# Moving operand tiles and weight-slab slots to other byte offsets within 512

## The reference

```python
h = h + 0.5 * swiglu(rmsnorm(h), w_gate, w_up, w_down)          # FFN_DIM = 2816
h = h + mixer(rmsnorm(h))   # three branches, gated and summed, then @ w_out:
#   gated linear attention (4 heads), Mamba-2 SSD (8 groups of 4 heads), chunked attention (16 heads)
h = h + 0.5 * swiglu(rmsnorm(h), w_gate2, w_up2, w_down2)
return rmsnorm(h)
```

## Time and profile before

| | before |
|---|---|
| median of three runs | 1852.97 us (1850.91 to 1854.07) |
| the profiled execution, its own time | 1850.31 us |
| its span, first to last instruction | 1848.5 us |
| what lies around the span | 1.8 us |
| mean granted TensorE clock | 0.996 |
| PE busy | 1817.7 us (98%), 9852 matmuls |
| PEld busy | 1499.5 us (81%), 9852 loads |
| DVE, ACT, POOL busy | 961.3, 622.2, 115.5 us |
| DMA | 89 GB/s on average |

### The profile page before, as it was taken

How to read it: one execution, slowest core, us unless ns; L and a number is a source line. 1 busy time by engine, 2 the same in 40 slices (tenths; PEclk the granted TensorE clock), 3 DMA queues, 4 the chain that set the end, 5 groups by cost and what they waited for, 6 DMA issues and landing times.

```text
span 1848.5 us, 26276 instructions
## 1 busy us (share of the span) xinstructions
PE 1817.7 (98%) x9852; PEld 1499.5 (81%) x9852; DVE 961.3 (52%) x1360; ACT 622.2 (34%) x986; POOL 115.5 (6%) x109
## 2 busy tenths in 40 slices
PE   7999999999999999999999999999999999999997
PEld 5888888887888888788888888887888888888885
DVE  6444443379888888532544445555334544444333
ACT  4323222234444444332233244443222323232221
POOL 4111100001101100000000000000000011111000
PEclk9999999999999999999999999999999999999998
DMA  4332223331222222222222222222232223232331
GB/s 157 100 97 96 98 95 102 102 98 62 70 68 68 79 68 68 80 92 95 88 85 75 82 89 85 84 91 69 92 98 95 91 94 99 94 99 92 109 104 58
DMA packets 47353, 164.92 MB, mean 89 GB/s; under 512 B 5520, under 2 KB 6672, under 8 KB 47296
## 3 DMA queue, kind: packets, MB, share of 16 engines
q1 hardware_dynamic: 43584, 158.10, 26.4%
q10 hardware_dynamic: 3712, 6.03, 1.1%
HBM read 162.01 MB, written 2.10 MB: 89 GB/s over the span
## 4 chain that ended last, share of the span: by engine, by line
PE 75%; issue 19%; DVE 3%; POOL 1%; ACT 1%; DMA 0%; POOLq 0%; DVEq 0%; SPq 0%; ACTq 0%
PE G L536 37%; PE G L578 12%; PE I L536 9%; PE G L552 7%; PE I L898 1%; POOL hid L458 1%; PE I L932 1%; PE I L908 1%; PE I L707 1%; PE I L715 1%; PE G L765 1%; DVE UL L1495 1%; PE I L725 1%; PE I L868 0%; PE I L872 0%
## 5 line engine op out<-in xcount | busy, mean ns | idle before, releaser
L1479 DVE TENSOR_TENSOR WL<-RAW,WH 128x1024 fp32r<-128x1024 f32 x297 | 374.1, 1262 | 309.6 <-ACT WH L1027 300.7
L1027 ACT CAST WH<-RAW 128x1024 fp32r<-128x1024 f32 x297 | 309.3, 1046 | 240.6 <-PE I L536 131.9
L536 PE MATMUL G<-UH,WH 128*128 128x512 f32 x696 | 172.9, 390 | 0.0
L536 PE MATMUL G<-UH,WL 128*128 128x512 f32 x696 | 171.9, 389 | 0.0
L536 PE MATMUL G<-UL,WH 128*128 128x512 f32 x696 | 171.8, 389 | 0.0
L536 PEld LDWEIGHTS G<-UH,WH 128*128 128x128 f32 x696 | 130.6, 188 | 28.0 <-issue 1.0
L536 PEld LDWEIGHTS G<-UL,WH 128*128 128x128 f32 x696 | 130.7, 188 | 27.1
L536 PEld LDWEIGHTS G<-UH,WL 128*128 128x128 f32 x696 | 130.7, 188 | 27.1
L536 PE MATMUL G<-NH,WH 128*128 128x512 f32 x448 | 115.5, 399 | 0.0
L536 PE MATMUL G<-NL,WH 128*128 128x512 f32 x448 | 113.6, 395 | 0.0
L536 PE MATMUL G<-NH,WL 128*128 128x512 f32 x448 | 113.6, 395 | 0.0
(11 more groups left out here) (309 smaller groups left out, 2551.4 us busy)
## 6 DMA issues: line engine op xcount, KB each, us to landing
RAW<-in_slabs SPq DMA_DIRECT2D x297, 512.0 KB, 3.3
h<-in_x SPq DMA_DIRECT2D x4, 512.0 KB, 6.4
bias<-in_rel ACTq DMA_DIRECT2D x16, 128.0 KB, 3.1
out_y<-h ACTq DMA_DIRECT2D x8, 256.0 KB, 2.2
bias<-in_rel ACTq DMA_DIRECT2D x16, 112.0 KB, 2.6
cst<-in_cst SPq DMA_DIRECT2D x1, 168.0 KB, 3.6
ut<-in_wgk SPq DMA_DIRECT2D x3, 32.0 KB, 8.3
```

The lines of the kernel that those rows point to most:

```text
L536: ins = mm(dst, W[:, n.slot, (k - k0) * P:(k - k0 + 1) * P], R[:, k, :], start=begin and which == 0 and k == k0, stop=end and which == 2 a ...
L1027: nc.scalar.copy(WH[:, n.slot, :], RAW[:, n.slot, :]).then_inc(split_hi, 1)
L1479: V.tensor_tensor(WL[:, n.slot, :], RAW[:, n.slot, :], WH[:, n.slot, :].bitcast(F32), ALU.subtract).then_inc(split_lo, 1)
```

## The change

Nothing is computed differently; instructions, their order and their semaphores stay. Only places in SBUF change:

- Every slot of `WH` and `WL` gets 16 spare elements (64 bytes) behind it. Slots are 4160 bytes apart: `WH` slots begin at 128, 192 and 256 in 512, `WL` slots at 320, 384 and 448.
- A tensor `offset` of 32 elements fills up to the next 512 bytes.
- Small tensors move (`four_eps`, `DAH`, and the attention tiles `PT2`, `mx`, `ngm`, `rs`, `rc`), so that everything fits, and so that the large operand tiles behind the tables begin at 128 in 512 in place of 160: `NH`, `NL`, `HH`, `HL`, `SL`, `AH`, `AL`, `MH`, `ML`, and also `ut`, `MSH`, `MSL`, `WGK` and the working tiles. `after_r` goes from 192 to 160 and `LR` from 352 to 320. `UH`, `UL`, `GH`, `GL`, `SH` and `RAW` stay at 128.

```diff
+STEP = 16
-        WH = sb("WH", [P, RING, SLAB], F32R)
-        WL = sb("WL", [P, RING, SLAB], F32R)
+        WH = sb("WH", [P, RING, SLAB + STEP], F32R)
+        WL = sb("WL", [P, RING, SLAB + STEP], F32R)
+        sb("offset", [P, 128 - 6 * STEP])
...
-        four_eps = sb("four_eps", [P, TT])
...
+        late = ExitStack()
+        PT2 = sb("PT2", [P, 2, 256], F32, late)
+        mx = sb("mx", [P, 2, TT], F32, late)
+        ngm = sb("ngm", [P, 2, TT], F32, late)
+        rs = sb("rs", [P, 2, TT], F32, late)
+        rc = sb("rc", [P, 2, TT], F32, late)
+        late.close()
         SC = sb("SC", [P, 32, HS])
...
+        DAH = sb("DAH", [P, TT * HS], F32R, prep)
         prep.close()
...
-        DAH = sb("DAH", [P, TT * HS], F32R, w)
+        four_eps = sb("four_eps", [P, TT], F32, w)
...
-        PT2 = sb("PT2", [P, 2, 256], F32, w)
-        mx = sb("mx", [P, 2, TT], F32, w)
-        ngm = sb("ngm", [P, 2, TT], F32, w)
-        rs = sb("rs", [P, 2, TT], F32, w)
-        rc = sb("rc", [P, 2, TT], F32, w)
...
-                nc.scalar.copy(WH[:, n.slot, :], RAW[:, n.slot, :]).then_inc(split_hi, 1)
+                nc.scalar.copy(WH[:, n.slot, 0:SLAB], RAW[:, n.slot, :]).then_inc(split_hi, 1)
...
-                V.tensor_tensor(WL[:, n.slot, :], RAW[:, n.slot, :], WH[:, n.slot, :].bitcast(F32),
+                V.tensor_tensor(WL[:, n.slot, 0:SLAB], RAW[:, n.slot, :], WH[:, n.slot, 0:SLAB].bitcast(F32),
                                 ALU.subtract).then_inc(split_lo, 1)
```

## The result

| | before | after |
|---|---|---|
| median of 16 runs each | 1851.27 us (1850.18 to 1854.07) | 1855.49 us (1854.71 to 1856.33) |
| ratio after / before | | 1.0022, 95% interval 1.0014 to 1.0030 |
| the profiled execution, its own time | 1850.31 us | 1854.89 us |
| its span | 1848.5 us | 1853.1 us |
| mean granted TensorE clock | 0.996 | 0.995 |

The change costs 4.2 us. The forecast was 1872 us, +19.0: the right side, inside the range, but more than four times the size. (Of the 16.5 us between 1872 and 1855.5, 1.7 come from the median of before, 1852.97 when the prediction was made and 1851.27 now.)

A forecast was written before the change was run, and what follows sets the result against it. PE, busy throughout, was taken to bound the kernel through its step length. +6.1 us (512 columns) and +12.9 (256 columns) made +19.0 on 1850.3, 1869.3; with 2.7 for the median, 1872 us, range 1848 to 1895.

The forecast's parts named there:

- The two-port rule: Trainium skill's rule that moving operand and weight load have independent read ports; by it the change is worth nothing.
- Step 2: 512-column matmuls: moving the operands alone brings 3392 of them from 233.5 to 226.7 ns, -23.1 us.
- the 64-byte rival: Pattern repeats every 64 bytes: 512-column steps settle at 226.7 ns, 256-column form +2.7 us; 1833 us; chance 14%.
- Step 3: 512-column matmuls: spare bytes spread the leads over 0 to 320; net with the operands' move, +6.1 us.
- lead: Stationary operand's place in 512 less the moving one's; claimed 229.0 ns at 0 and 64, 233.5 from 128 to 320.
- Step 4: 256-column matmuls of line 578: 1493 of them, off lead 0, rise to 126.6 ns; +12.9 us.
- The inference of a period of 512: Weight load and moving stream meet about once in 512 bytes, so the pattern repeats after 512, not 64, 128 or 256.
- The 256-column form doesn't care: Rival: line 578 is unmoved, its +12.9 us term nothing; +6 us in all, 1859 us; chance 16%.
- dearer: Rival: 4866 matmuls put at the dear level take 238 ns, 4.5 ns more; +22 us, 1894 us; chance 12%.
- no meeting: Rival: some middle leads of the 512-column form step at 213.3 ns; below 1805 us; chance 4%.
- Nothing: Rival: nothing to measure, as gains and losses cancel or addresses play no part; 1853 us; chance 9%.

The follow-up runs named there:

- pad_only: Changed kernel with its padded slots, but the operands behind the tables left at 160 as before; 1861.32 us, ratio 1.0052 to the kernel before.
- align_only: Changed kernel without the spare bytes: operands moved to 128, slots unpadded; 1833.77 us, ratio 0.9902 to the kernel before.
- hi0_lo64: Changed kernel without slot padding, 16 spare elements between WH and WL instead: WH slots at lead 0, WL at lead 64; 1853.13 us.
- hi0_lo192: Changed kernel without slot padding, 48 spare elements between WH and WL instead: WH slots at lead 0, WL at lead 192; 1840.46 us.

## Why the prediction was right or wrong

**What bounds the kernel: right.** All versions keep their work and their clock (0.993 to 0.996), the steps with waits in them add up to the same within 4 us, and the time follows the step. Between the two extremes, 1833.8 and 1876.6 us, nothing differs but addresses.

**The two-port rule: the trace disagrees, as said, and the runs now show it.** The Trainium skill, page TensorE: Matmul & The Clock Gate, section "Step-by-step: what each phase is for", has the weight load take nothing from the running matmul, because each has its own read port. Moving tiles alone took 1% off the kernel (0.9902), and the price goes by the place of the one operand less that of the other (`pad_only`). The same page, section "Back-to-back issue gap", gives N / 2.4 + 2.5 ns for the gap of an isolated matmul; an estimate by it is 215.8 ns for 512 columns. No settled step with 512 columns was under 226.7 here, where each matmul brings its own weight load.

**Step 2, moving the operands: right in the steps.** -23.1 us was forecast, -22.4 measured in `align_only`. The 256-column form gave +2.8, as the 64-byte rival had it (+2.7). What I left out is that waits give back some 3.6 us of the 19.6: the span fell by 16.0.

**Step 3, the spare bytes in the 512-column form: near in its sum, by errors that cancel.** +6.1 us forecast, +4.1 measured. Against what the slots measured:

- lead 0: 229.0 forecast, 229.0 measured; reading it from the earlier trace rows held.
- lead 64: 229.0 forecast, 233.4 measured: 1349 x 4.4 = 5.9 us too little. The failing reading is "its nearest row is +32, which is cheap": cheapness was taken from the shortest duration in a group of 389/482/775. Both 32 and 64 settle at 233.3.
- lead 192: 233.5 forecast, 228.6 measured, 675 x 4.9 = 3.3 us too much; lead 256: 233.5 against 231.1, 1.6 us too much. The second is lead 0, unsettled in a run of eight behind lead 64.
- lead 128 (232.8) and 320 (233.4): as forecast but for 0.9 us.
- The slots have no equal shares. The 40 slabs of the 256-column form always fall in slots 1 and 2, so slot 0, the cheap one, has 99 of the 257 others. That gives some 1.3 of the remaining 2 us.

By settled prices, with these shares, the changed kernel would have a mean of 99/257 x 227.4 + 79/257 x (231.1 + 232.9) = 230.2 ns, and the kernel before has (2680 x 226.7 + 3392 x 233.3) / 6072 = 230.4. So the set of leads that the change brings is no dearer than the old one. The measured means are 231.2 and 230.5: the changed kernel pays 1.0 ns a step for switching the lead within and between slabs, the size seen in `hi0_lo64` and `hi0_lo192`, where before paid 0.1. (0.9 ns more by 5960 steps is 5.4 us, less 0.2 x 5960 = 1.2 of the settled prices: the +4.1.) This split is worked out, from settled prices measured one by one. It was not shown by a kernel with the same leads and no switches, which can't be built.

**Step 4, the 256-column form: this is the step that failed.** +12.9 us forecast, -1.3 measured; this term is 14.2 of the 14.4 us between the +19.0 of the sum and the +4.6 of the span (step 3 is 2.0 more, and the SSD rounds, which had no term, give 1.8 the other way with the rest). Its size was 119.8 + 6.8 ns, the price that the other form pays, carried over because "the extra falls in the time of the weight load, which both forms have whole". Not one D brings the mean of this form above 119.9 ns. It even ranks them otherwise: D 0, best with 512 columns, is worst here, together with 96. Beyond the columns alone (213.3 and, at 2.4 GHz, 256 / 2.4 = 106.7 ns) D 0 costs the same 13 ns in both forms, which fits the argument; but going from D 0 to 64 adds 6.6 ns with 512 columns and takes away 2.3 with 256. So it is the extra of the other places that doesn't carry over from one form to the other. The lower bound that I had written down (118.3, costing nothing more) was still a little high. The share of lead 0 was wrong as well (none of the WH slabs, since slot 0 isn't used), but that hardly matters at prices between 117.3 and 119.9.

**The inference of a period of 512: wrong.** Lines 822 and 679 were to exclude 64, 128 and 256. The row of line 822 does exclude 64: 320 would be 0 there, and it was dear, as the runs confirm. But 128 and 256 were both excluded by "288 would be 32", and so by the misread 32. For 128 the runs bear the conclusion out all the same (232.7 ns at lead 128, 226.7 at 0); for 256 they refute it. One bad reading thus made both the wrong period and the wrong price of lead 64. The picture of a load that meets the stream once in 512 bytes falls with it.

**The rivals.** "The 256-column form doesn't care" (1859 us) was the mechanism that decided, and its change is the nearest: +6 against the 4.2 measured. That it comes so near is in part luck, since its +6 is step 3 with errors that cancel. Of the 3.5 us between 1859 and 1855.5, 1.7 are again the median of before. The 64-byte repeat is refuted by lead 64, "dearer" at 238 and "no meeting" at 213.3 by the table: all settled 512-column steps lie between 226.7 and 234.2. "Nothing" had the nearest time, 1853 us. As "addresses play no part" it is refuted by `align_only`; as "gains and losses cancel" it is nearly what happened: of the 22.4 us won on the 512-column steps by moving the operands, the spare bytes gave back 26.5. That the two don't cancel fully the interval of 1.0014 to 1.0030 shows, narrowly.

**Not settled.** Why these places cost what they cost. The runs show a dependence on one difference modulo 256, and at 128 and 208 on something besides; they don't show what meets what, nor why even the best place is 13.4 ns above the 213.3 that the columns take. The 96-partition row of line 822 wasn't tried by itself. Of the +1.7 us in the SSD rounds only the place is known: the first `XTE`,`BK` group has a mean of 435 ns after and 404 in `align_only`. It doesn't go by D: it has 402 ns at lead 64 and 435 at lead 320, which are the same D modulo 256.

## What to carry to other kernels

Where PE is full and each matmul brings its own weight load, put the streamed tiles and the weight slots at the same remainder by 256 bytes and keep it the same over all ring slots and both precision parts: that was worth 1.0% here, with nothing else changed than places. Pad slots by 256 bytes or by nothing, measure the settled step of each matmul form apart and not by analogy, and read it from a run of many equal matmuls, never from a shortest duration.

## What the runs showed of the hardware

- The step of back-to-back fp32r matmuls depends on the place of the slab slot less that of the activation, modulo 256: 226.7 to 234.2 ns with 512 columns, 114.9 to 119.9 ns with 256. The two forms rank the places differently; of the nine places tried 192 is the only one cheap for both.
- At 128 and 208 the same tiles at the same places settle at two different steps in one execution: 232.4 and 233.3 ns, 233.3 and 231.7.
- It is not smooth: 226.7 at 0, 233.3 at 224, 232.3 at 208, 228.9 at 192.
- Inside a settled run the steps repeat in a short pattern: 226, 227, 227 ns at 0, 231 and 236 in turn at 64, 226, 229, 232 at 192, and seven steps between 228 and 241 at 128 (first feed-forward block).
- A new lead needs about eight matmuls to settle (230 ns, then 226.3); two switches in a slab cost some 24 ns.
